# Block moves of a hybrid mixer: issued by ScalarE in its written order, by way of a DRAM scratch of two halves

## The chip, the cores and the metric

The kernel runs on one core of one Trainium2 chip. The metric is the device time of one execution in microseconds; it is given as the median of the runs shown. Times inside a profile are microseconds from the first instruction. TensorE (PE) multiplies matrices, VectorE (DVE), ScalarE (ACT) and GpSimd (POOL) work on elements, SyncE (SP) issues DMAs only.

## The reference

One layer of an encoder block for 256 tokens of width 2048, in float32:

```python
h  = rms_norm(x, pre_mix_g)
P  = h @ w_in                        # u, B, C (1024 each), c_q (768), c_kv (512), k_rope (64)
yA = group_rms_norm(B * conv3_causal(C * u))
q  = rms_norm(c_q) @ w_uq            # 8 heads of 128 + 64
kv = rms_norm(c_kv) @ w_ukv          # 8 heads of 128 + 128
o  = chunk_causal_attention(q_nope, rope(q_rope), k_nope, rope(k_rope), v)
yB = group_rms_norm(o)               # one group for each head
x  = x + rms_norm(concat(yA, yB) @ w_o, post_mix_g)
x  = x + rms_norm(square(relu(rms_norm(x) @ w_up)) @ w_down, post_mlp_g)
```

## The kernel before

**Products.** All weights are streamed once. Each product is made of three matmuls: weights and activations are split into a high part and a rest (`w_hi`, `w_lo`, `xT_hi`, `xT_lo`), and hi*hi, lo*hi and hi*lo are added. The unit is a quad: four chunks of 128 weight rows by 512 columns, 1 MB, loaded by SyncE into one of four `raw` slots (L605). A quad has two halves of two chunks. ScalarE copies a half to `w_hi` (L1005), VectorE subtracts to get `w_lo` (L1305), TensorE does 6 matmuls for each chunk (L725 to L727), 12 for a half. A half is split four halves ahead of its use: the split waits for the end of the half four earlier (`half_used`), and it stands in ScalarE's and VectorE's order at the odd chunk of that earlier half.

**One written order.** `plan()` (L76) writes a single list of steps. Every engine walks the whole list and does its own part of each step, so the list fixes the order on each engine. The first three strips of the input projection make the latents (`lat`), then come 24 quads of u, c and b columns. Before each of their chunks, number `sub`, `between(sub)` (L130) puts the small work of the head pairs and of the convolution. Pair p (0 to 3) begins at step 8 + 16p: kv product, q product (+4), kq turn (+6), `qrT` (+9), `q_order` (+13), scores (+15), probsT (+19), pv (+22), sum of squares and normalisation of o (+24, +25), o turn (+26), `o_split` (+36). So the o turn of pair p stands at step 34 + 16p, and `q_order` and scores of pair p+1 at 37 + 16p and 39 + 16p. Convolution turns stand at 38 and 54.

**Moves of blocks.** Twelve times a 256-token tile has to be transposed without TensorE: 2 latent strips, 4 times k and q, 4 times o, 2 convolution strips. VectorE transposes 32x32 blocks into the one buffer `blk` (`turn_batch`, L1329, `blk_turned`), after the batch before has been stored (`blk_stored`). Then four DMAs store `blk` into `mix_rows` in DRAM (L634), and a fifth reads it back with the blocks in their places (L647, `blk_landed`). SyncE does all this in `move_batch`, called after the load of the fourth quad after the turn. Its waits stand in the same queue as the weight loads. The scratch holds one batch, so the stores wait until the batch before has landed.

**Who waits for a landing.** `lat_split` (L1106) makes cqT from the latents. `q_order` on ScalarE (L1138) waits for the kq batch, copies q into order and raises `qT_ready`; TensorE's score matmuls (L909, L914) wait for it. `o_split` (L1162) and the convolution's steps (L1189) wait for theirs, with many steps in between. In ScalarE's order one split stands between step 35 + 16p and the `q_order` of step 37 + 16p.

Of the kernel before, what the change touches and what calls it, by code (L numbers as in the profile page):

```python
# [27 lines left out]
F32 = mybir.dt.float32  # L28
# [18 lines left out]
BLK = 32  # L47
# [23 lines left out]

S_CONV, S_OUT = 3, 9
CONV_PARTS = "ucb" * 2


def plan():  # L76
# [6 lines left out]
        quads[n] = dict(kind=kind, **kw)  # L83
        return n

    def turn(kind, i):

        batches.append((kind, i, len(quads) + 4))
        steps.append((kind + "_turn", i, len(batches) - 1))

    def products(n, into=steps, then=None):

# [11 lines left out]
    for s in range(3):  # L104
        for q in range(4):
            n = quad("in", strip=s, q=q, nk=4, width=min(W, LAT - s * W), col=LAT0 + s * W,
                     first=q == 0, last=q == 3)
            for k in range(4):
                steps.append(("mm", n, k))
                if s == 0 and q < 2 and k % 2:  # L110
                    c = 8 + 4 * q + 2 * (k // 2)
                    steps += [("xT", c, 0), ("xT", c + 1, 0)]
                if (s, q, k) == (1, 1, 1):
                    steps.append(("x_stats", 0, 0))
                if (s, q, k) == (1, 2, 0):
                    steps.append(("lat_out", 0, lat_ends[0]))
                if (s, q, k) == (1, 2, 1):
                    turn("lat", 0)
                if (s, q, k) == (2, 0, 1):
                    turn("lat", 1)  # L120
                    steps.append(("lat_squares", 0, 0))
                if (s, q, k) == (2, 1, 0):
                    steps.append(("lat_split", 0, 0))
        lat_ends[s] = n
        if s:
            steps.append(("lat_out", s, n))
    steps += [("lat_squares", 1, 0), ("rotatedate", 0, 0)]


    def between(sub):  # L130
        if sub == 2:
            steps.append(("latT", 0, 0))
        if sub == 1:
            steps.append(("lat_split", 1, 0))
        if sub == 6:
            steps.append(("krT", 0, 0))
        if sub in (38, 54):
            turn("conv", sub // 54)
        for p in range(PAIRS):
            at = sub - 8 - 16 * p  # L140
            if at == 0:
                n = quad("kv", p=p, nk=4, width=W)
                products(n)
                steps.append(("kv_out", p, n))
            if at == 4:
                for part in range(2):
                    n = quad("q", p=p, part=part, nk=3, width=QW)
                    products(n)
                steps.append(("q_out", p, n))
            if at == 6:  # L150
                turn("kq", p)
            if at == 26:
                turn("o", p)
            for when, what, h in [(9, "qrT", 0), (13, "q_order", 0), (15, "scores", 0), (15, "scores", 1),
                                  (19, "probsT", 0), (19, "probsT", 1), (22, "pv", 0), (24, "o_squares", 0),
                                  (25, "o_norm", 0), (36, "o_split", 0)]:
                if at == when:
                    steps.append((what, p, h))
        for c in range(4):
            for half, t, norm in [(0, 70 + 6 * c, 8), (1, 98 + 4 * c, 5)]:  # L160
                if sub == t:
                    steps.append(("convT", half, c))
                if sub == t + 2:
                    steps.append(("conv_square", half, c))
                if sub == t + norm:
                    steps.append(("conv_norm", half, c))

    sub = 0
# [73 lines left out]
    n = up(0, 3)  # L242
# [58 lines left out]

def hybrid_block(nc, t, out):
    steps, tail, quads, batches = plan()
    BATCH = {(kind, i): n for n, (kind, i, _) in enumerate(batches)}
    NQ_TAIL = min(n for what, n, _ in tail if what == "mm")
    NQ_ALL = max(quads) + 1
    LOOP = range(2, FF_STRIPS - 2)
# [3 lines left out]
    with ExitStack() as ctx:  # L311
# [197 lines left out]
            k = m - Q_RANK // P  # L509
            return yT_hi[:, KV_AT + k], yT_lo[:, KV_AT + k], G_KV + k  # L510

        mix_rows = nc.dram_tensor("mix_rows", (4, BLK, 4, 8 * BLK), F32, kind="Internal").ap()

        def landed(batch):
            return 16 * (BATCH[batch] + 1)
# [86 lines left out]
        def _(sp):  # L602
# [18 lines left out]
                        sp.dma_start(aT_raw[BLK * q:BLK * (q + 1), g], a_blk[BLK * g:BLK * (g + 1), q]  # L621
                                     ).then_inc(aT_landed, 16)

            def move_batch(m):

                kind, i, _ = batches[m]
                size = 4 * BLK if kind == "o" else 8 * BLK
                sp.wait_ge(blk_turned, m + 1)
                if m:

                    sp.wait_ge(blk_landed, 16 * m)
                for g in range(4):
                    src = blk[BLK * g:BLK * (g + 1)].rearrange("p q b c i -> p q (b c i)")[:, :, 0:size]
                    sp.dma_start(mix_rows[:, :, g, 0:size].rearrange("q r n -> r q n"), src).then_inc(blk_stored, 16)  # L634
                if kind == "kq":
                    sp.wait_ge(latT_lo_ready, 2)
                    if i:
                        sp.wait_ge(scores_done, 2 * i)
                elif kind == "lat" and i:
                    sp.wait_ge(latT_lo_ready, i)  # L640
                elif kind == "o":
                    sp.wait_ge(latT_lo_ready, 3)
                    sp.wait_ge(kr_ready, 4)
                    if i:
                        sp.wait_ge(oT_lo_ready, i)
                sp.wait_ge(blk_stored, 64 * (m + 1))
                sp.dma_start(landing(kind, i), mix_rows[:, :, :, 0:size].rearrange("q r g n -> (q r) g n")  # L647
                             ).then_inc(blk_landed, 16)

            def load_x(tb):  # L650
                sp.dma_start(x_in[:, tb], x_dram[:, tb]).then_inc(x_landed, 16)

# [10 lines left out]
            for n in range(RAW, NQ):  # L663
                z = quads[n]

                sp.wait_ge(lo_ready, 2 * (n - RAW) + 2)
                load_quad(n % RAW, quad_source(n), z["nk"], z["width"])
                if n in (5, 6):
                    load_x(n - 5)
                if n == 7:  # L670
                    sp.dma_start(ident[:], t["ident"]).then_inc(ident_landed, 16)
                    sp.dma_start(cos_t[:], t["cos"]).then_inc(tables_landed, 16)
                    sp.dma_start(sin_t[:], t["sin"]).then_inc(tables_landed, 16)
                for m, (_, _, after) in enumerate(batches):
                    if after == n:
                        move_batch(m)
                if n == RESIDUAL_QUAD:

                    sp.wait_ge(oT_lo_ready, PAIRS)
                    sp.dma_start(g_post_mix[:], t["post_mix_g"].to_broadcast([P, D])).then_inc(g_mix_landed, 16)  # L680
                    sp.dma_start(x_res[:], x_dram).then_inc(x_res_landed, 16)
# [316 lines left out]
        def _(act):  # L998
# [58 lines left out]
            def step(what, a, b):  # L1057
# [64 lines left out]
                elif what == "q_out":  # L1122
# [5 lines left out]
                    for tb in range(TB):  # L1128
                        ins = nc.scalar.activation(q_sb[:, tb], ps[:, 4 + tb, 0:QW], ACT.Copy,  # L1129
                                                   scale=rstd_lat[:, tb:tb + 1])  # L1130
                    ins.then_inc(q_ready, 1)
                elif what == "q_order":
                    act.wait_ge(blk_landed, landed(("kq", a)))
                    if a:
# [697 lines left out]
```

## Time and profile before

| | before |
|---|---|
| median of 3 runs | 1068.28 us (1066.87 to 1068.4) |
| the profiled execution | 1067.39 us |
| its span, first to last instruction | 1065.6 us |
| TensorE busy | 1053.6 us, 99% |
| VectorE busy | 695.2 us, 65% |
| ScalarE busy | 515.9 us, 48% |
| mean granted TensorE clock | 0.997 |

The profile has a page, with busy times and the costliest groups of instructions, and a trace that can be asked for timelines of an engine, for tables of busy time by stretch, and for waits. In a timeline row "x4" means four instructions in a row merged, with their time in common; the brackets give the idle time before and what ended it. "SPq" and "ACTq" are the instructions by which SyncE and ScalarE issue DMAs; their time is that of the issue, not of the transfer, and does not count as busy. Matmuls overlap: their pitch is the distance of their starts. PEclk 1.00 is the full clock of 2.4 GHz.

### The profile page before, as it was taken

The numbers are of one execution on the slowest core, as the hardware profiler recorded it, in microseconds if no ns is written. First come the engines' busy times: TensorE is split into PE (matmuls) and PEld (weight loads), VectorE is DVE, ScalarE is ACT, GpSimd is POOL, SyncE is SP. The second block draws the span as 40 slices with busy tenths as digits, with TensorE's granted clock in tenths as the row PEclk, the third lists the DMA queues.
The fourth block names the chain that finished last, engine by engine and source line by source line (L and its number), as shares of the span: only waits on it lengthen the run. The fifth ranks groups of instructions, "written<-read, shape, count | busy, mean of one in ns | idle before, by whom it ended". The sixth has DMA issues, their size and how long they took to land.

```text
span 1065.6 us, 13494 instructions
## 1 busy us (share of the span) xinstructions
PE 1053.6 (99%) x4794; PEld 877.0 (82%) x4794; DVE 695.2 (65%) x785; ACT 515.9 (48%) x666; POOL 80.7 (8%) x94
## 2 busy tenths in 40 slices
PE   9999999999999999999999999999999999999996
PEld 7898888888888788888888888888888888888885
DVE  6475566679975876575575665756657656565666
ACT  7575545565544664444444444444444444444443
POOL 0011022110000310000000000000000000000003
PEclk9999999999999999999999999999999999999998
DMA  9786667864586465776666756666576665676562
GB/s 345 261 300 218 201 184 272 271 221 151 204 307 198 125 212 157 237 226 197 209 184 212 231 172 232 196 199 212 170 236 216 203 211 159 220 232 190 181 242 79
DMA packets 125619, 225.78 MB, mean 212 GB/s; under 512 B 8464, under 2 KB 30096, under 8 KB 124816
## 3 DMA queue, kind: packets, MB, share of 16 engines
q1 hardware_dynamic: 125152, 224.89, 64.7%
q10 hardware_dynamic: 432, 0.44, 0.1%
q8 instruction: 21, 0.34, 0.1%
q14 instruction: 14, 0.11, 0.0%
HBM read 210.08 MB, written 7.34 MB: 204 GB/s over the span
## 4 chain that ended last, share of the span: by engine, by line
PE 85%; issue 11%; DVE 2%; POOL 1%; DMA 1%; ACT 0%; SPq 0%; DVEq 0%; POOLq 0%; ACTq 0%
PE ps L725 28%; PE ps L727 28%; PE ps L726 28%; DMA raw<-in_w_in 1%; PE ps L748 1%; POOL acc L1666 0%; DVE w_lo L1305 0%; PE ps L909 0%; PE ps L914 0%; POOL x_res L1777 0%; POOL x_res L1751 0%; ACT w_hi L1005 0%; SPq L656 0%; DVE conv_s L1532 0%; DVEq L311 0%
## 5 line engine op out<-in xcount | busy, mean ns | idle before, releaser
L1305 DVE TENSOR_TENSOR w_lo<-raw,w_hi 128x1024 fp32r<-128x1024 f32 (+2 forms) x382 | 465.2, 1226 | 318.9 <-ACT w_hi L1005 316.8
L1005 ACT ACTIVATE w_hi<-raw 128x1024 fp32r<-128x1024 f32 (+2 forms) x382 | 395.8, 1038 | 460.7 <-PE ps L727 456.3
L725 PE MATMUL ps<-w_hi,xT_hi 128*128 128x512 f32 (+1 forms) x792 | 308.5, 390 | 0.6 <-DVE xT_lo L1406 0.5
L727 PE MATMUL ps<-w_lo,xT_hi 128*128 128x512 f32 (+1 forms) x792 | 305.9, 386 | 0.0
L726 PE MATMUL ps<-w_hi,xT_lo 128*128 128x512 f32 (+1 forms) x792 | 305.8, 386 | 0.0
L725 PE MATMUL ps<-w_hi,yT_hi 128*128 128x512 f32 x672 | 263.1, 391 | 0.0
L727 PE MATMUL ps<-w_lo,yT_hi 128*128 128x512 f32 x672 | 261.6, 389 | 0.0
L726 PE MATMUL ps<-w_hi,yT_lo 128*128 128x512 f32 x672 | 261.4, 389 | 0.0
L725 PEld LDWEIGHTS ps<-w_hi,xT_hi 128*128 128x128 f32 x792 | 148.7, 188 | 31.9 <-issue 2.0
L727 PEld LDWEIGHTS ps<-w_lo,xT_hi 128*128 128x128 f32 x792 | 148.6, 188 | 30.0
L726 PEld LDWEIGHTS ps<-w_hi,xT_lo 128*128 128x128 f32 x792 | 148.8, 188 | 28.7
L727 PEld LDWEIGHTS ps<-w_lo,yT_hi 128*128 128x128 f32 x672 | 126.1, 188 | 26.5
L726 PEld LDWEIGHTS ps<-w_hi,yT_lo 128*128 128x128 f32 x672 | 126.2, 188 | 26.1
L725 PEld LDWEIGHTS ps<-w_hi,yT_hi 128*128 128x128 f32 x672 | 126.1, 188 | 25.9
L1379 DVE TENSOR_TENSOR acc<-acc,ps 128x1024 f32<-128x1024 f32 x58 | 70.8, 1220 | 18.4 <-PE ps L727 17.5
L1685 POOL TENSOR_TENSOR a_sb<-a_sb 128x1024 f32<-128x1024 f32 x16 | 30.3, 1895 | 583.0 <-ACT a_sb L1035 583.0
L1035 ACT ACTIVATE a_sb<-ps,rstd_x 128x512 f32<-128x512 f32 x32 | 20.2, 683 | 19.9 <-PE ps L727 19.9
L1325 DVE TENSOR_TENSOR yT_lo<-aT_raw,yT_hi 128x512 fp32r<-128x512 f32 x32 | 20.6, 683 | 0.0
L1350 DVE STREAM_TRANSPOSE a_blk<-a_sb 128x512 f32<-128x512 f32 x30 | 19.5, 687 | 0.0
L1044 ACT ACTIVATE yT_hi<-aT_raw 128x512 fp32r<-128x512 f32 x32 | 18.2, 615 | 1.5 <-DVE aT_raw L1360 1.5
L1672 POOL TENSOR_TENSOR rope_c<-q_sb,cos_t 128x128 f32<-128x128 f32 x8 | 8.6, 1073 | 114.6 <-ACT q_sb L1129 114.3
L727 PE MATMUL ps<-w_lo,cqT_hi 128*128 128x384 f32 x48 | 16.1, 335 | 0.0
(155 smaller groups left out, 425.3 us busy)
## 6 DMA issues: line engine op xcount, KB each, us to landing
raw<-in_w_up SPq DMA_DIRECT2D x64, 1024.0 KB, 5.5
raw<-in_w_down SPq DMA_DIRECT2D x64, 1024.0 KB, 5.3
raw<-in_w_in SPq DMA_DIRECT2D x28, 1024.0 KB, 6.0
raw<-in_w_o SPq DMA_DIRECT2D x16, 1024.0 KB, 5.0
aT_raw<-a_blk SPq DMA_DIRECT2D x240, 32.0 KB, 1.9
raw<-in_w_uq SPq DMA_DIRECT2D x8, 576.0 KB, 4.9
mix_rows<-blk SPq DMA_DIRECT2D x32, 128.0 KB, 2.4
raw<-in_w_ukv SPq DMA_DIRECT2D x4, 1024.0 KB, 5.3
```

The lines of the kernel that those rows point to most:

```text
L725: nc.tensor.matmul(dst, x_hi, hi, start=first, stop=False)
L726: nc.tensor.matmul(dst, x_lo, hi, start=False, stop=False)
L727: mm = nc.tensor.matmul(dst, x_hi, lo, start=False, stop=last)
L748: mm = nc.tensor.transpose(ps[:, bank, i * P:(i + 1) * P], src, ident[:])
L1005: nc.scalar.activation(w_hi[:, slot, 0:size], raw[:, raw_slot, first:first + size], ACT.Copy).then_inc(hi_ready, 1)
L1035: ins = nc.scalar.activation(a_sb[:, tb], ps[:, bank + tb], ACT.Relu, scale=rstd_x2[:, tb:tb + 1])
L1044: ins = nc.scalar.activation(turned(yT_hi, at, tb), blocked(tb), ACT.Copy)
L1305: nc.vector.tensor_tensor(w_lo[:, slot, 0:size], raw[:, raw_slot, first:first + size], f32(w_hi[:, slot, 0:size]), ALU.subtract).then_inc( ...
L1325: ins = nc.vector.tensor_tensor(turned(yT_lo, at, tb), blocked(tb), f32(turned(yT_hi, at, tb)), ALU.subtract)
L1350: ins = nc.vector.transpose(a_blk[:, :, tb].rearrange("p q c i -> p c q i"), a_sb[:, tb].rearrange("p (c q i) -> p c q i", c=4, q=4))
L1379: nc.vector.tensor_tensor(m, m, ps[:, bank:bank + 2], ALU.add).then_inc(acc_added, 1)
L1685: nc.gpsimd.tensor_tensor(a, a, a, ALU.mult).then_inc(a_ready, 1)
```

## The change

SyncE's `move_batch` goes. The list of steps gets two new steps for each batch, `move_store` and `move_read`, and ScalarE carries them out where they stand. For a turn at step `at` the store stands at `at + 1`, the read at `at + 4` (kq), `at + 5` (o) or `at + 6` (conv), each ahead of everything else of that step. For the two latent batches the places are written by hand. The store waits for the turn and issues four DMAs; the read waits as before for the landing place to be free, for the batch before to have landed and for its own stores, and issues one. The scratch `mix_rows` has two halves used in turn, and the wait for the landing of the batch before moves from the store to the read.

```diff
+MOVE = {"kq": 4, "o": 5, "conv": 6}
...
-    def turn(kind, i):
-
-        batches.append((kind, i, len(quads) + 4))
+    moves = {}
+
+    def turn(kind, i, at=None):
+
+        batches.append((kind, i))
         steps.append((kind + "_turn", i, len(batches) - 1))
+        if at is not None:
+            moves.setdefault(at + 1, []).append(("move_store", len(batches) - 1, 0))
+            moves.setdefault(at + MOVE[kind], []).append(("move_read", len(batches) - 1, 0))
...
+                for b, when in enumerate([((1, 2, 3), (1, 3, 3)), ((2, 0, 3), (2, 2, 2))]):
+                    if (s, q, k) in when:
+                        steps.append((("move_store", "move_read")[when.index((s, q, k))], b, 0))
...
     def between(sub):
+        steps.extend(moves.pop(sub, []))
...
-        mix_rows = nc.dram_tensor("mix_rows", (4, BLK, 4, 8 * BLK), F32, kind="Internal").ap()
+        mix_rows = nc.dram_tensor("mix_rows", (2, 4, BLK, 4, 8 * BLK), F32, kind="Internal").ap()
...
-                for m, (_, _, after) in enumerate(batches):
-                    if after == n:
-                        move_batch(m)
...
+                elif what == "move_store":
+                    kind, i = batches[a]
+                    size = 4 * BLK if kind == "o" else 8 * BLK
+                    act.wait_ge(blk_turned, a + 1)
+                    for g in range(4):
+                        src = blk[BLK * g:BLK * (g + 1)].rearrange("p q b c i -> p q (b c i)")[:, :, 0:size]
+                        act.dma_start(mix_rows[a % 2, :, :, g, 0:size].rearrange("q r n -> r q n"), src
+                                      ).then_inc(blk_stored, 16)
+                elif what == "move_read":
...
+                    if kind == "kq":
+                        act.wait_ge(latT_lo_ready, 2)
+                        if i:
+                            act.wait_ge(scores_done, 2 * i)
+                    elif kind == "lat" and i:
+                        act.wait_ge(latT_lo_ready, i)
+                    elif kind == "o":
+                        act.wait_ge(latT_lo_ready, 3)
+                        act.wait_ge(kr_ready, 4)
+                        if i:
+                            act.wait_ge(oT_lo_ready, i)
+                    if a:
+
+                        act.wait_ge(blk_landed, 16 * a)
+                    act.wait_ge(blk_stored, 64 * (a + 1))
+                    act.dma_start(landing(kind, i), mix_rows[a % 2, :, :, :, 0:size].rearrange("q r g n -> (q r) g n")
+                                  ).then_inc(blk_landed, 16)
```

## Rows read from the trace of the kernel before

**Rows 1.** The page's part 1: busy us (share of the span) xinstructions.
```profile
PE 1053.6 (99%) x4794; PEld 877.0 (82%) x4794; DVE 695.2 (65%) x785; ACT 515.9 (48%) x666; POOL 80.7 (8%) x94
```

**Rows 2.** Windows: stretch, its us, busy us of PE, PEld, DVE, ACT, POOL; PEclk, DMA share, GB/s.
```profile
44.00:340.00 296.00, 296.00 (x1445) 251.04 (x1444) 203.82 (x304) 158.27 (x251) 29.24 (x53) 1.00 0.68 228
```

**Rows 3.** Timeline of ScalarE, 0 to 4 us: start, us, engine, line, operation, [idle before].
```profile
1.72 0.39 ACTq L1050 DMA_DIRECT2D xT_raw<-in_xT  x1
...
2.95 0.20 ACT L1055 ACTIVATE rstd_m<-ones 128x2 f32<-128x2 f32 x1
```

**Rows 4.** Timeline of SyncE's queue, pair 1: groups of four stores.
```profile
137.95 1.78 SPq L634 DMA_DIRECT2D mix_rows<-blk  x4
...
146.12 3.37 SPq L634 DMA_DIRECT2D mix_rows<-blk  x4
```

**Rows 5.** Timeline of VectorE, pair 1.
```profile
138.75 1.23 DVE L1305 TENSOR_TENSOR w_lo<-raw,w_hi 128x1024 fp32r<-128x1024 f32 x1 [0.83 <-ACT w_hi L1005]
...
145.38 0.70 DVE L1334 STREAM_TRANSPOSE blk<-o_sb 128x512 f32<-128x512 f32 x1
```

**Rows 6.** Timeline of ScalarE, pair 1: a split, and q_order.
```profile
137.66 1.06 ACT L1005 ACTIVATE w_hi<-raw 128x1024 fp32r<-128x1024 f32 x1 [3.02 <-PE ps L727]
...
145.14 0.72 ACT L1138 ACTIVATE lat<-kqT 128x256 f32<-128x256 f32 x2 [0.72 <-DMA kqT<-mix_rows]
```

**Rows 7.** Timeline of TensorE, pair 1: the first score matmuls.
```profile
147.24 1.47 PE L909 MATMUL ps<-kqT,lat 128*128 128x128 f32 x8
```

**Rows 8.** Timelines of VectorE and TensorE, pairs 2 and 3.
```profile
176.96 1.23 DVE L1305 TENSOR_TENSOR w_lo<-raw,w_hi 128x1024 fp32r<-128x1024 f32 x1 [0.83 <-ACT w_hi L1005]
...
182.28 0.70 DVE L1334 STREAM_TRANSPOSE blk<-o_sb 128x512 f32<-128x512 f32 x1
...
185.44 1.47 PE L909 MATMUL ps<-kqT,lat 128*128 128x128 f32 x8
...
220.48 0.70 DVE L1334 STREAM_TRANSPOSE blk<-o_sb 128x512 f32<-128x512 f32 x1
...
223.65 1.47 PE L909 MATMUL ps<-kqT,lat 128*128 128x128 f32 x8
```

**Rows 9.** Timelines of ScalarE and TensorE, pair 0: q_order and scores.
```profile
107.28 0.73 ACT L1138 ACTIVATE lat<-kqT 128x256 f32<-128x256 f32 x2 [1.06 <-DMA kqT<-mix_rows]
...
109.03 1.47 PE L909 MATMUL ps<-kqT,lat 128*128 128x128 f32 x8
```

**Rows 10.** Timelines of all engines, 51 to 64 us: the latent batches.
```profile
51.79 1.25 ACT L1020 ACTIVATE lat<-ps,rstd_x 128x512 f32<-128x512 f32 x2
...
52.41 0.34 SPq L647 DMA_DIRECT2D kqT<-mix_rows  x1
...
55.77 1.99 SPq L634 DMA_DIRECT2D mix_rows<-blk  x4
...
55.99 1.70 ACT L1106 ACTIVATE cqT_hi<-kqT,gains 128x256 fp32r<-128x256 f32 x4
...
59.83 2.68 DVE L1305 TENSOR_TENSOR w_lo<-raw,w_hi 128x640 fp32r<-128x640 f32 x3
...
61.50 0.31 PE L725 MATMUL ps<-w_hi,xT_hi 128*128 128x320 f32 x1
...
63.38 0.34 SPq L647 DMA_DIRECT2D kqT<-mix_rows  x1
```

**Rows 11.** Timelines of VectorE and TensorE, 249 to 259 us: the last o batch.
```profile
249.59 0.70 DVE L1334 STREAM_TRANSPOSE blk<-o_sb 128x512 f32<-128x512 f32 x1
...
255.66 2.35 DVE L1305 TENSOR_TENSOR w_lo<-raw,w_hi 128x1024 fp32r<-128x1024 f32 x2
...
258.07 0.39 PE L725 MATMUL ps<-w_hi,xT_hi 128*128 128x512 f32 x1
```

**Rows 12.** Windows around TensorE's last matmul, columns as in rows 2.
```profile
1056.00:1060.00 4.00, 0.57 (x3) 0.14 (x1) 3.23 (x6) 1.02 (x3) 3.25 (x3) 1.00 0.66 262
1060.00:1061.00 1.00, 0.00 (x0) 0.00 (x0) 1.00 (x2) 0.00 (x0) 0.00 (x0) 0.54 0.00 0
```

More of the change, by code:

```diff
@@ L137, in between @@
         if sub in (38, 54):
-            turn("conv", sub // 54)
+            turn("conv", sub // 54, sub)
         for p in range(PAIRS):
@@ L150, in between @@
             if at == 6:
-                turn("kq", p)
+                turn("kq", p, sub)
             if at == 26:
-                turn("o", p)
+                turn("o", p, sub)
             for when, what, h in [(9, "qrT", 0), (13, "q_order", 0), (15, "scores", 0), (15, "scores", 1),
@@ L303, in hybrid_block @@
     steps, tail, quads, batches = plan()
-    BATCH = {(kind, i): n for n, (kind, i, _) in enumerate(batches)}
+    BATCH = {(kind, i): n for n, (kind, i) in enumerate(batches)}
     NQ_TAIL = min(n for what, n, _ in tail if what == "mm")
@@ L622, in move_blocks @@
                                      ).then_inc(aT_landed, 16)
[L624 to L648, printed above, removed]
             def load_x(tb):
@@ L1131, in step @@
                     ins.then_inc(q_ready, 1)
+                elif what == "move_store":
[7 more added lines that the diff above has]
+                elif what == "move_read":
+                    kind, i = batches[a]
+                    size = 4 * BLK if kind == "o" else 8 * BLK
+                    if kind == "kq":
[14 more added lines that the diff above has]
+                                  ).then_inc(blk_landed, 16)
                 elif what == "q_order":
```

## The prediction

> **What bounds the kernel now.** I read the page first: TensorE is busy 1053.6 of 1065.6 us, ScalarE 515.9 [rows 1]. Then the table of windows over the stretch in which the twelve batches of blocks are moved: from 44 to 340 us TensorE is busy 296.00 of 296.00 us at full clock, ScalarE 158.27, VectorE 203.82 [rows 2]. So there TensorE alone sets the end, nothing in that stretch can be gained, and every microsecond in which it stands still is a microsecond of the result. Third, the timelines of SyncE, ScalarE, VectorE and TensorE around each batch, to see how much room lies between a thing that TensorE needs and the moment it needs it. Matmuls of 512 columns start 0.227 us apart in TensorE's timeline, so a half quad (two chunks, 12 matmuls) takes 2.72 us. A half is split four halves ahead: ScalarE waits for the end of half H, makes w_hi of H+4, VectorE then w_lo; TensorE asks for it three halves after H.
>
> **What goes from SyncE.** 48 stores and 12 reads leave its queue, and with them its waits for turns and landings. What stands behind them there are weight loads. In the stretch of rows 2 TensorE has no idle time at all, so earlier weights are worth nothing. I cost this at zero; the cover is the four raw slots, and if it were gone weights would only be earlier than now, so no loss either.
>
> **What comes to ScalarE: issue time.** The nearest rows are its own load at the start, 0.39 us, and SyncE's groups of four stores, 1.78 us [rows 3, 4]. So 12 x (4 x 0.44 + 0.4) = about 26 us of ScalarE, spread over some 210 us in which it is about half busy. By total it fits. A load was also issued at 1.72 us while the copy ahead of it in ScalarE's order ran only at 2.95 [rows 3]: an issue need not wait for work queued ahead to finish, only for its semaphores. What counts is therefore the order: a store at one step after the turn waits for VectorE's transposes, and VectorE runs several us behind TensorE. Behind the waiting store stand w_hi splits, and in three of the four head pairs the q_order copy, for which the score matmuls wait.
>
> **Pair 1 worked out.** (a) The kq turn is done when SyncE's stores start, 137.95, and four issues take 1.78 us [rows 4]. ScalarE reaches that step earlier (it is idle 3.02 us before its split at 137.66 [rows 6]), waits, issues until 139.73, and only then makes the split, 2.07 us late. (b) VectorE's w_lo at 138.75 [rows 5] follows that split, so it starts at 139.73 + 1.06 + 0.03 = 140.82, again 2.07 late. Behind it in VectorE's order stand the sum of squares of o, the normalisation (with GpSimd between them) and the o turn, a serial chain: the turn at 145.38 + 0.70 = 146.08 [rows 5] becomes 148.15. (c) The o stores now stand in ScalarE's order ahead of one split and of q_order. ScalarE waits till 148.15, issues 1.77 us (149.96), splits 1.06 (151.02), copies q in 0.73 (151.75) [rows 6]. (d) TensorE began the scores at 147.24 [rows 7], the instant its previous chunk was through; now 151.85. That is a stall of 4.6 us. The kq read is no part of it: its stores have landed when ScalarE comes to it, and its data were there by 145.14 [rows 6]. After the scores ScalarE also waits for the conv turn and issues four stores before it takes the exponentials: by the same steps they end 7.2 us after the scores begin. Weights split before last till three halves and the scores are through (2.4 + 1.36 + 5.44 = 9.2 us), so I put nothing there.
>
> **Pairs 2 and 3.** Same steps; VectorE has no conv product in the chain, so the turn stood earlier against the scores. Pair 2: the w_lo behind the kq turn, 176.96, moves by the same 2.07 to 179.03; the end of the o turn, 182.98, to 185.05; plus 1.77 + 1.06 + 0.73 + 0.05 gives 188.65 against 185.44: 3.2 us. Pair 3: turn end 221.18 + 2.07, plus 3.6, gives 226.85 against 223.65: 3.2 us [rows 8].
>
> **Pair 0** has no o batch ahead of it. The kq stores delay a split and u's copy, the read's stores have landed before, and q_order ran at 107.28 to 108.01 with the scores at 109.03 [rows 9]: 1.0 us of room, against at most 1.3 us of delay if the read had to wait for the splits to finish. I take 0, bound 0.3.
>
> **The two latent batches.** The first batch's read stood at 52.41, and the copy of strip 1 at 51.79 on ScalarE comes behind it now, 1.0 us later; the second turn, which needs that copy, is 1.0 later too (stores from 56.8 where they stood at 55.77). They take 2.0 us, and lat_split, which ran at 55.99, starts at 58.8: 2.8 us later. VectorE's half of it and the first w_lo behind it (59.83 + 0.82 = 60.65) come to 63.5, while TensorE wants that half at 61.50 [rows 10]. Stall 2.0 us. Bounds: 1.0, if the first group of stores lands sooner, so that strip 1's copy is not held up, and 4.0 if both groups go as slowly as the slowest, 3.37 [rows 4].
> On the queues: the stores from 55.77 were followed by their read only 7.6 us later, with a megabyte of weights on the same queue ahead of them [rows 10]. The Trainium skill, "DMA: Bandwidth & Descriptors", Queues, rings and completion order, says that each DMA engine goes round between the queues that have work, a packet at a time; blocks on ScalarE's queue would then not stand behind weights. By that rule the latent stall would be 1.0 and the sum 1 us less; by the row it is 2.0, which I keep.
>
> **The last o batch.** Its turn ends at 250.29. ScalarE issues till 252.1, and its next split is ready at 253.2, where VectorE now has it long before it wants it. In VectorE's order follow that half's w_lo (1.2 us), a convolution's reciprocal and gain (3.0) and the next half's w_lo (1.2), which so ends at 258.6; it started at 255.66 and ended at 256.8. TensorE asks for that half at 258.07 [rows 11]. Stall 0.5, bounds 0 and 1.7, since VectorE is nearly full till 300 us and keeps the lateness. The conv batches' turns are followed by nothing urgent: 0 beside what stands under pair 1.
>
> **Sum.** 2.0 + 0 + 4.6 + 3.2 + 3.2 + 0.5 = 13.5 us. The profiled execution took 1067.39 us (span 1065.6 and 1.8 around it), so 1080.9 by it; it lies 0.9 below the median of the three runs, 1068.28, which gives 1081.8. Nothing is given back later: outside that stretch TensorE's idle time is 12 us in all [rows 1], at the start and the end.
>
> **Rivals.**
> (A) The clock falls in a stall. After the last matmul, at 1056.18, the clock was still 1.00 up to 1060 and 0.54 in the slice from 1060 to 1061 [rows 12]: it drops to its lower level after some 3.5 us of idleness. The stall of pair 1 is longer, the other two about as long. At 1.2 GHz the 0.227 us pitch doubles. No row shows how long it stays low; if as long as it took to fall, each fall costs 1.75 us. One fall: 1083.6; three: 1087. For: 4.6 is above 3.5. Against: 3.2 is below. Chance 0.2.
> The Trainium skill, "TensorE: Matmul & The Clock Gate", Part 1, tells the same: a gate halves the clock once the array has been idle and opens after it has been busy for a while. The rows agree on the fall; the rise is in no row here.
> (B) Issues on ScalarE are slow because SyncE issues weights beside them. The slowest group took 3.37 us [rows 4]; 1.6 more in each of three pairs: 13.5 + 4.8, 1086.6. Chance 0.12.
> (C) VectorE is not shifted by the kq stores (the split gets ahead of them), and only the o stores block: 2.5 + 1.1 + 1.1, and 1 for the latents: 1074. Against it is the written order. Chance 0.12.
> (D) Not slower. The point is the o turn: if it ended 4.6 us earlier against the scores (before 143.6 in pair 1), ScalarE would pass the stores without holding q_order. That could be if the o chain, with SyncE out of the way, ran ahead. Time 1068.3, with no stall left. Against it: the chain is released by ScalarE's splits and by TensorE, and SyncE appears nowhere in it. Chance 0.08.
> Main case: 0.48.
>
> **Numbers.** Forecast 1081.8. The range runs from (C), less 1 us for latents that cost nothing, 1073, to three clock falls or slow issues with a little more in the latent and last batches, 1090; only (D) and a sum of both bad cases is left out. Measurements of this kernel tell 0.2% (2.1 us) from no change. Faster 0.03, same 0.06, slower 0.91.
>
> **What would show it.** TensorE idle just before the score matmuls of line 909 by 4.6, 3.2 and 3.2 us in pairs 1, 2 and 3 and none in pair 0; ScalarE's o stores starting as VectorE's o turn ends, with q_order after them; the w_lo behind each kq turn 2.1 us later against TensorE; an idle time of 2 us in strip 2; the clock below 1.00 in pair 1 for (A). I would be wrong if q_order ran ahead of the o stores, if the stalls were at weights instead of scores, or if TensorE showed none.

## The result, and the profile after

The changed kernel takes 1092.62 us (median of 4 runs, 1091.2 to 1093.26) where the kernel before takes 1067.91 beside it (4 runs): a ratio of 1.023 (95% interval 1.0217 to 1.0243), 24.7 us more. Forecast was 1081.8, with a range to 1090: the direction was right, the size was not, and the time lies outside the range.

| | before | after |
|---|---|---|
| the profiled execution | 1067.39 us | 1091.2 us |
| its span | 1065.6 us | 1089.4 us |
| TensorE busy | 1053.6 us | 1060.2 us |
| TensorE idle in the span | 12.0 us | 29.2 us |
| mean granted clock | 0.997 | 0.993 |

So 23.8 us of span come from two sources: 17.2 us in which TensorE stands still, and 6.6 us by which the same 4794 matmuls are busy longer. The page of the changed kernel: part 1, which answers to [rows 1], and the line of part 3 for ScalarE's queue (packets, MB, share), on which the blocks now travel:

```profile
PE 1060.2 (97%) x4794; PEld 880.3 (81%) x4794; DVE 695.3 (64%) x785; ACT 514.4 (47%) x666; POOL 80.6 (7%) x94
...
q10 hardware_dynamic: 10608, 10.92, 3.5%
```

Two lines of TensorE's waits (us in total, times, longest) hold 16.2 us of the idle time:

```profile
PE ps L890 <- issue: 11.1, 3, 4.6
PE ps L706 <- DVE w_lo L1314: 5.1, 4, 3.4
```

Windows of the changed kernel, columns as in [rows 2], show where it is. Before, TensorE was busy through all of this stretch at full clock [rows 2]:

```profile
44.00:64.00 20.00, 18.75 (x107) 16.86 (x106) 8.40 (x11) 9.68 (x18) 0.58 (x1) 1.00 0.74 213
64.00:92.00 28.00, 24.63 (x116) 21.00 (x115) 18.72 (x33) 16.76 (x28) 3.59 (x9) 0.94 0.65 215
128.00:172.00 44.00, 39.44 (x192) 33.11 (x191) 24.43 (x39) 17.46 (x29) 6.39 (x11) 0.96 0.60 189
172.00:212.00 40.00, 36.76 (x179) 30.70 (x178) 22.82 (x39) 18.19 (x30) 6.39 (x11) 0.96 0.65 214
212.00:264.00 52.00, 48.71 (x248) 41.27 (x247) 33.27 (x57) 27.41 (x47) 7.44 (x12) 1.00 0.69 223
```

The first two are strip 2, where the latent batches are moved: 1.25 + 3.37 = 4.6 us idle. The other three hold the score matmuls of pairs 1, 2 and 3: 4.56, 3.24 and 3.29. The clock column is below 1.00 in three of the five. TensorE's timeline has the same stalls one by one (start, us, operation, idle before and what ended it); the last two rows are those behind the last o batch:

```profile
59.87 0.42 PE L706 MATMUL ps<-w_hi,xT_hi 128*128 128x320 f32 x1 [0.85 <-DVE w_lo L1314]
62.29 0.41 PE L706 MATMUL ps<-w_hi,xT_hi 128*128 128x320 f32 x1 [0.40 <-DVE w_lo L1314]
67.69 0.64 PE L706 MATMUL ps<-w_hi,xT_hi 128*128 128x320 f32 x1 [3.37 <-DVE w_lo L1314]
159.59 2.90 PE L890 MATMUL ps<-kqT,lat 128*128 128x128 f32 x8 [4.56 <-issue]
202.76 2.00 PE L890 MATMUL ps<-kqT,lat 128*128 128x128 f32 x8 [3.24 <-issue]
246.04 1.55 PE L890 MATMUL ps<-kqT,lat 128*128 128x128 f32 x8 [3.29 <-issue]
281.16 0.50 PE L706 MATMUL ps<-w_hi,xT_hi 128*128 128x512 f32 x1 [0.49 <-DVE w_lo L1314]
298.24 0.67 PE L938 MATMUL ps<-conv_s,ones 128*128 128x256 f32 x2 [0.40 <-ACT conv_s L1204]
```

Eight score matmuls took 1.47 us before [rows 7]; behind the stall of pair 1 they take 2.90. Slices of 2 us around it, same columns, show why: the clock falls near the end of the stall and comes back some 3.4 us later (a slice at c spends 2(1-c)/0.5 us low: 0.64 + 2.00 + 0.76).

```profile
156.00:158.00 2.00, 0.00 (x0) 0.00 (x0) 0.00 (x0) 0.18 (x1) 0.00 (x0) 1.00 0.42 90
158.00:160.00 2.00, 0.41 (x2) 0.44 (x3) 1.09 (x1) 2.00 (x4) 0.00 (x0) 0.84 0.20 42
160.00:162.00 2.00, 2.00 (x8) 1.59 (x7) 1.67 (x3) 0.44 (x1) 0.00 (x0) 0.50 0.57 161
162.00:164.00 2.00, 2.00 (x13) 1.17 (x12) 1.30 (x6) 0.00 (x0) 0.00 (x0) 0.81 0.99 346
```

ScalarE's timeline in pair 1 tells why `q_order` comes late. The o turn (VectorE's, 155.20 + 0.70) ends at 155.90; only then are the four stores issued, then the split, then q:

```profile
145.59 1.78 ACTq L1119 DMA_DIRECT2D mix_rows<-blk  x4
...
155.93 1.79 ACTq L1119 DMA_DIRECT2D mix_rows<-blk  x4
157.82 1.06 ACT L986 ACTIVATE w_hi<-raw 128x1024 fp32r<-128x1024 f32 x1 [8.34 <-DMA mix_rows<-blk]
158.78 0.71 ACT L1147 ACTIVATE lat<-kqT 128x256 f32<-128x256 f32 x2
```

TensorE was through with its weights at 155.03. What stands in the way is thus the order on ScalarE, as forecast. The latent batches are another matter. ScalarE's timeline of the first of them:

```profile
48.66 3.12 ACTq L1119 DMA_DIRECT2D mix_rows<-blk  x4
56.62 0.34 ACTq L1139 DMA_DIRECT2D kqT<-mix_rows  x1
57.07 1.27 ACT L1001 ACTIVATE lat<-ps,rstd_x 128x512 f32<-128x512 f32 x2 [3.81 <-DMA mix_rows<-blk]
```

SyncE's timeline beside it, three loads of weights from 45.65 to 54.61; they start at 45.65, 49.37 and 54.25, so the last two go out between the first store and the read:

```profile
45.65 8.96 SPq L615 DMA_DIRECT2D raw<-in_w_in  x3
```

The read in the table of DMAs from 45 to 62 us (KB, us from issue to landing):

```profile
kqT<-mix_rows ACTq DMA_DIRECT2D x1, 512.0 KB, 6.3
```

From the first store to the read 8.0 us pass, and the read lands 6.3 us later. In the kernel before, SyncE's timeline has the stores here:

```profile
47.80 2.77 SPq L634 DMA_DIRECT2D mix_rows<-blk  x4
```

and the same table of DMAs has the read:

```profile
kqT<-mix_rows SPq DMA_DIRECT2D x1, 512.0 KB, 3.3
```

Its read followed at 52.41 [rows 10], 4.6 us after the first store, and SyncE issued no weights in between. In the changed kernel they go out beside the stores, ahead of the read. Loads behind a read do no such harm: the second latent read of the changed kernel, at 68.05, had none issued in the 5.8 us ahead of it and one 0.34 us behind it, and landed in 3.5 us; the read of before at 52.41 had loads 0.39 and 0.87 us behind it.

### The profile page after: what moved, and what is told of

Same layout as the page of the kernel before. It is cut to its first block, busy times and chain, and to the rows that moved or that the text cites. A ratio compares the mean times of both kernels' runs of the same rounds, so it can differ in the third digit from the quotient of the medians.

```text
span 1089.4 us, 13489 instructions
## 1 busy us (share of the span) xinstructions
PE 1060.2 (97%) x4794; PEld 880.3 (81%) x4794; DVE 695.3 (64%) x785; ACT 514.4 (47%) x666; POOL 80.6 (7%) x94
## 4 chain that ended last, share of the span: by engine, by line
PE 81%; issue 12%; DVE 2%; ACT 1%; DMA 1%; POOL 1%; ACTq 0%; SPq 0%; DVEq 0%; POOLq 0%
PE ps L706 26%; PE ps L708 26%; PE ps L707 26%; PE ps L890 1%; DMA raw<-in_w_in 1%; DVE w_lo L1314 1%; PE ps L729 1%; DMA mix_rows<-blk 1%; POOL acc L1675 0%; ACT w_hi L986 0%; PE ps L895 0%; ACTq L1119 0%; POOL x_res L1786 0%; POOL x_res L1760 0%; DVE cqT_lo L1348 0%
## 5 line engine op out<-in xcount | busy, mean ns | idle before, releaser
L890 PE MATMUL ps<-kqT,lat 128*128 128x128 f32 (+1 forms) x32 | 7.9, 402 | 11.1 <-issue 11.1
```

What stands on the lines that cost most here:

```text
L890: nc.tensor.matmul(ps[:, (6, 7)[h], cols], qT[:, tb, h], kT, start=tb == 0, stop=False, skip_group_check=True)
```

## The experiments

Theory at the start: (T1) the order on ScalarE makes the stalls, by the o stores ahead of `q_order` and by the kq stores that make the o turn late; (T2) SyncE's waits had held weight loads back, and freed loads run against the blocks; (T3) the clock falls in the stalls. The rival to T1 is the time of issuing on ScalarE as such, that to T2 the order of the latent steps, that to T3 that the slow matmuls have another cause. The kernels `only_o`, `only_kq` and `lat_sync` keep SyncE's old `move_batch` for the kinds named in `BY_SYNC`; all of them keep the scratch of two halves.

**only_o: the four o batches by ScalarE, all others by SyncE.**

```diff
+BY_SYNC = ('lat', 'kq', 'conv')
...
-        if at is not None:
+        if at is not None and kind not in BY_SYNC:
...
+                for m, (kind, _, after) in enumerate(batches):
+                    if after == n and kind in BY_SYNC:
+                        move_batch(m)
```

> Only the four o batches are issued by ScalarE, at the changed kernel's places; latent, kq and conv batches stay with SyncE. Theory (order: the o stores stand ahead of q_order and hold it until VectorE's o turn): the chain without the kq shift of 2.07 us gives idle times of TensorE ahead of the scores of 2.5, 1.1 and 1.1 us in pairs 1 to 3, no fall of the clock, and 0.5 us at the last batch: 5 us above before, 1073. Rival 1 (time of issue: each batch costs in proportion): 4 of 12 batches cost a third of 24.7, 8 us, 1076, with no idle time tied to scores. Rival 2 (the kq stores alone do it): 1068.

Measured 1075.85 us, ratio 1.007 (1.0053 to 1.0087). Windows of pairs 1 and 2:

```profile
128.00:172.00 44.00, 41.58 (x203) 35.21 (x202) 27.18 (x44) 19.95 (x33) 6.40 (x11) 0.96 0.67 218
172.00:212.00 40.00, 38.89 (x196) 32.97 (x196) 25.18 (x43) 19.52 (x33) 6.40 (x11) 1.00 0.72 231
```

TensorE's timeline in pairs 2 and 3:

```profile
191.61 1.55 PE L920 MATMUL ps<-kqT,lat 128*128 128x128 f32 x8 [1.11 <-issue]
231.44 1.55 PE L920 MATMUL ps<-kqT,lat 128*128 128x128 f32 x8 [1.39 <-issue]
```

The stalls are 2.42, 1.11 and 1.39 (4.9 in all), against 2.5, 1.1 and 1.1 by the prediction's steps without the shift by the kq stores. Above the forecast lies first the clock: 0.96 in pair 1, after a stall of only 2.42 us. Not all of the 3.6 us by which TensorE is busy longer is the clock's, though. From the scores of pair 2 to those of pair 3, with no fall, 39.83 us pass, 1.39 of them the stall; that leaves 38.44, where it was 38.21 before [rows 8]. So a stall costs some 0.2 us beside its own length.

**only_kq: the kq batches by ScalarE, all others by SyncE** (the edit above with `BY_SYNC = ('lat', 'o', 'conv')`).

> Only the four kq batches are issued by ScalarE, at the changed kernel's places; the rest stays with SyncE. Theory: VectorE's o turns come 2.07 us later, as in the changed kernel, but nobody on TensorE's side waits for them, so no idle time ahead of the scores: within 1 us of before, 1068. Rival 1 (time of issue): a third of 24.7, 1076. Rival 2 (the kq stores hold q_order by themselves): idle times ahead of the scores in pair 0 too, 3 us or more in all, 1071 and up.

Measured 1068.09 us over 10 runs, ratio 1.0003 (0.9993 to 1.0012). The window of pair 1 has no idle time:

```profile
128.00:172.00 44.00, 44.00 (x222) 37.62 (x221) 30.45 (x47) 22.29 (x36) 6.88 (x12) 1.00 0.69 230
```

although in VectorE's timeline the o turn came at 147.79, where it stood at 145.38 [rows 5]:

```profile
147.79 0.70 DVE L1373 STREAM_TRANSPOSE blk<-o_sb 128x512 f32<-128x512 f32 x1
```

The issue time of 20 DMAs on ScalarE costs nothing by itself: that rival falls. The kq stores do harm only where the o stores wait for the turn that they make late: 0 and 4.9 us of stall alone, 11.1 together.

**o_late: the o store three steps later, its read two.**

```diff
-MOVE = {"kq": 4, "o": 5, "conv": 6}
+MOVE = {"kq": 4, "o": 7, "conv": 6}
+STORE = {"kq": 1, "o": 4, "conv": 1}
...
-            moves.setdefault(at + 1, []).append(("move_store", len(batches) - 1, 0))
+            moves.setdefault(at + STORE[kind], []).append(("move_store", len(batches) - 1, 0))
```

> The changed kernel with the o stores three steps later, at +4 after the turn and so behind the next pair's q_order, and the o reads at +7. Theory: the three idle times ahead of the scores (4.56, 3.24, 3.29 us, together 11.1) go, and with them two falls of the clock, 1.7 us each. In their place VectorE's conv turn waits for the o stores and the conv stores come later, ahead of the exponentials: some 1.5 us of waits at weights in pair 1. 1092.6 - 11.1 - 3.4 + 1.5 = 1079.6. Rival (the time of issue or the number of waits on ScalarE counts, not the place): no change, 1092.

Measured 1085.74 us, ratio 1.0167 (1.015 to 1.0184). No stall is left at the scores, but others came. VectorE's timeline in pair 1, and TensorE's:

```profile
163.59 1.31 DVE L1344 STREAM_TRANSPOSE blk<-u_sb 128x512 f32<-128x512 f32 x2 [5.70 <-DMA mix_rows<-blk]
```

```profile
170.78 0.80 PE L707 MATMUL ps<-w_hi,xT_hi 128*128 128x512 f32 x1 [4.06 <-DVE w_lo L1315]
```

The conv turn stands behind the o turn and needs `blk` empty. It now waited 5.70 us for the o stores; the softmax behind it on VectorE, and the splits behind that, came late. So a store can stand too late as well as too early, since there is one `blk`. The expectation had this wait, but at some 1.5 us of stalls in pair 1, and no fall of the clock; it was 4.06 us with a fall behind it, and further stalls of 1.48 and 1.53 us stand at 213.59 and 284.76.

**kq_late: the kq store one step later**, behind the split (`STORE = {"kq": 2, "o": 1, "conv": 1}`).

> The changed kernel with the kq stores one step later, at +2 after the turn, behind the split that they stood ahead of. Theory: that split is no longer late, VectorE's o turn comes 2.07 us earlier against TensorE, and the idle times ahead of the scores become 2.5, 1.1 and 1.1 us; two falls of the clock go too: 1092.6 - 6.4 - 3.4 = 1082.8. Rival (the o turn is late for another cause, such as DMAs beside it): idle times as in the changed kernel, 1092.

Measured 1083.05 us, ratio 1.0139 (1.0122 to 1.0156). TensorE's waits, and its timeline in pair 1:

```profile
PE ps L891 <- issue: 4.8, 4, 2.4
```

```profile
158.00 1.61 PE L891 MATMUL ps<-kqT,lat 128*128 128x128 f32 x8 [2.39 <-issue]
```

The stalls at the scores go from 11.1 to 4.8 us (0.32 in pair 0, then 2.39, 1.05, 1.06), those of `only_o`. The 2 us by which the kq stores delay a split, and with it the o turn, are thereby shown in each pair. That the time meets the 1082.8 expected is in part luck: of the two falls of the clock that were to go, the one in pair 1 stayed (0.96 from 128 to 172, behind 2.39 us), and the profiled execution is only 7.5 us below that of the changed kernel, where 9.8 were expected.

**lat_sync: only the two latent batches back to SyncE** (`BY_SYNC = ('lat',)`).

> The changed kernel with the two latent batches back at SyncE; kq, o and conv batches stay with ScalarE. Theory (parts add up): the idle times of TensorE in strip 2, 0.85 + 0.40 + 3.37 us, go, and the fall of the clock there, 1.7 us by the other falls; the score idle times stay: 1092.6 - 4.6 - 1.7 = 1086.3. Rival (the latent batches only shift work that is late anyway): under 2 us of gain, 1091.

Measured 1086.43 us, ratio 1.0169 (1.0146 to 1.0192). Windows, columns as in [rows 2]:

```profile
44.00:92.00 48.00, 48.00 (x256) 42.84 (x255) 29.33 (x47) 29.43 (x48) 3.59 (x9) 1.00 0.76 246
128.00:172.00 44.00, 39.44 (x185) 32.63 (x184) 25.13 (x40) 17.26 (x30) 6.39 (x11) 0.92 0.62 194
172.00:212.00 40.00, 36.75 (x169) 30.34 (x168) 22.65 (x38) 17.46 (x29) 6.39 (x11) 0.91 0.63 202
212.00:264.00 52.00, 48.73 (x237) 40.82 (x236) 33.26 (x56) 26.43 (x45) 7.43 (x12) 0.93 0.61 200
```

The 4.6 us in strip 2 are gone, the idle times of the pairs are within 0.02 us those of the changed kernel, and the clock fell in all three of them, for about 7 us each time (44 x 0.08/0.5, 40 x 0.09/0.5, 52 x 0.07/0.5). The median says less than it seems: two of the four runs took 1084 us and two, the profiled one among them, 1088.8, at granted clocks of 0.993 to 0.995 and of 0.989.

**gate: the changed kernel, but SyncE waits for the latent landings** after its 12th and 14th load, so that no more weights are under way beside them. This tells T2 from the order of the steps, which it leaves alone.

```diff
+LAT_LOADS = (11, 13)
...
+                for m, when in enumerate(LAT_LOADS):
+                    if n == when:
+                        sp.wait_ge(blk_landed, 16 * (m + 1))
```

> The changed kernel with one wait added on SyncE: after its 12th and 14th quad load it waits for the first and second latent batch to have landed, as it did by its own moves before. ScalarE still issues all moves. Theory (weights that SyncE no longer holds back run beside the first batch's stores and make them land 8 us after their issue instead of 4.6): the read goes out some 3 us earlier, the idle time in strip 2 is the 2.0 us of the prediction, the fall of the clock there goes: 1092.6 - 2.6 - 1.7 = 1088.3. Rival (ScalarE's own queue is slower by itself): idle time 4.6 as before, 1092.

Measured 1087.53 us, ratio 1.0196 (1.0179 to 1.0213). ScalarE's timeline, the table of DMAs from 45 to 62 us, and TensorE's timeline in strip 2:

```profile
48.27 2.76 ACTq L1123 DMA_DIRECT2D mix_rows<-blk  x4
52.87 0.34 ACTq L1143 DMA_DIRECT2D kqT<-mix_rows  x1
```

```profile
kqT<-mix_rows ACTq DMA_DIRECT2D x1, 512.0 KB, 3.1
```

```profile
64.11 0.41 PE L710 MATMUL ps<-w_hi,xT_hi 128*128 128x320 f32 x1 [2.12 <-DVE w_lo L1318]
```

From store to read 4.6 us again, as before the change, and the read lands in 3.1. The stall is 2.12, the 2.0 of the prediction. Of the 4.6 us in strip 2 the order thus makes 2.1, the weights beside the blocks 2.5. The clock stays at 1.00 in strip 2. Elsewhere it did not repeat the changed kernel: it fell in pair 1 for about 7 us (0.92 from 128 to 172), not in pair 2 behind a stall of 3.24 us, and in pair 3 behind one of 3.27.

**busy: 8, 6 and 6 dummy matmuls, whose product nothing uses, ahead of the scores of pairs 1 to 3**, while TensorE waits. It should keep the clock up.

The other waits of the scores move ahead of them (left out here).

```diff
+                    for _ in range((0, 8, 6, 6)[p]):
+                        nc.tensor.matmul(ps[:, 6, 3 * P:4 * P], ones[:], ones[:], start=True, stop=True)
                     pe.wait_ge(blk_landed, landed(("kq", p)))
                     pe.wait_ge(qT_ready, p + 1)
```

> The changed kernel with 8, 6 and 6 extra 128x128 matmuls of the ones tile on TensorE ahead of the scores of pairs 1, 2 and 3, in an unused part of the bank; they run while TensorE would stand idle, so the wait itself stays. Theory (the clock falls because TensorE is idle, and the low stretch after it costs some 1.7 us each in pairs 1 and 2): scores start at the same distance, clock 1.00 there, 1092.6 - 3.4 = 1089.2. Rival (the low clock costs nothing, its matmuls would wait anyway): 1092.6.

Measured 1093.29 us, ratio 1.0241 (1.0224 to 1.0258). It tells nothing of T3: the eight took 1.95 us in all, 2.82 of the wait stayed idle, and the clock fell all the same (0.50 in the slice from 160 to 162). I had sized them too small.

**busy2: the same with 18, 13 and 13.**

> As the kernel with 8, 6 and 6 extra matmuls, but with 18, 13 and 13. Eight of them took only 1.95 us there, 0.24 us each, and left TensorE idle for 2.8 us, and the clock fell all the same. Now 4.4, 3.2 and 3.2 us are filled, so almost nothing of the idle time stays. Theory (idleness makes the clock fall and the low stretch costs time): clock 1.00 in pairs 1 to 3, scores at the same distance, some 4 us less than the changed kernel, 1089. Rival (the low clock costs nothing): 1092.6.

Measured 1089.08 us, ratio 1.0199 (1.0181 to 1.0217). The window of pair 1, and TensorE's timeline in it (each dummy is two instructions):

```profile
128.00:172.00 44.00, 43.25 (x233) 37.35 (x232) 25.50 (x42) 17.62 (x30) 6.40 (x11) 1.00 0.61 188
```

```profile
155.82 4.18 PE L885 MATMUL ps<-ones 128*128 128x128 f32 x36
160.75 1.00 PE L892 MATMUL ps<-kqT,lat 128*128 128x128 f32 x5 [0.75 <-ACT lat L1149]
```

The clock is 1.00 in all three pairs, and the median is 3.5 us below that of the changed kernel. What a fall is worth is better read inside the profiles, since the runs of one kernel differ in their falls. The scores of pairs 1, 2 and 3 start at 160.75, 202.46 and 244.26 here, 41.71 and 41.80 us apart, where the changed kernel, with a fall behind each, has 43.17 and 43.28: 1.5 us for each fall. (The profiled executions are only 1.8 us apart, because strip 2 of this one has 1.1 us more of idle time.)

**halves: the kernel before with the scratch of two halves and the wait for the batch before moved to the read**, all by SyncE.

```diff
-                if m:
-                    sp.wait_ge(blk_landed, 16 * m)
...
-                    sp.dma_start(mix_rows[:, :, g, 0:size].rearrange("q r n -> r q n"), src).then_inc(blk_stored, 16)
+                    sp.dma_start(mix_rows[m % 2, :, :, g, 0:size].rearrange("q r n -> r q n"), src).then_inc(blk_stored, 16)
...
+                if m:
+                    sp.wait_ge(blk_landed, 16 * m)
```

> The kernel before, SyncE issuing everything, with the scratch of two halves alone and the wait for the landing of the batch before moved from store to read. Theory: batches rarely follow each other closely and TensorE has no idle time there: within 1 us of before, 1068. Rival (the second half or the moved wait costs, by slower landings): over 1070.

Measured 1067.66 us over 10 runs, ratio 1.0001 (0.9992 to 1.0011). This part of the change costs and gives nothing.

**placed: ten batches on ScalarE, at other places; the latents by SyncE.** The kq store stands behind the split (but in pair 0), the o store behind `q_order`, and the conv turns four steps later, so that they don't wait for `blk`.

```diff
-MOVE = {"kq": 4, "o": 5, "conv": 6}
+STORE = {"kq": 2, "o": 4, "conv": 1}
+MOVE = {"kq": 4, "o": 7, "conv": 5}
...
-        if sub in (38, 54):
-            turn("conv", sub // 54, sub)
+        if sub in (42, 58):
+            turn("conv", sub // 58, sub)
```

> Ten of twelve batches issued by ScalarE, in other places: kq stores at +2 after the turn (pair 0 at +1), o stores at +4 and their reads at +7, the conv turns at steps 42 and 58, behind the scores, with the store at +1 and the read at +5; the latent batches with SyncE. Theory (the place in ScalarE's order costs the time, not the issue): no idle time ahead of scores or weights, 1068 to 1069. Rival (some 22 us of issue time on ScalarE and the waits cost by themselves): above 1072.

Measured 1074.27 us, ratio 1.0062 (1.0044 to 1.008), not the 1068 to 1069 expected. Pairs 0 to 2 have at most 0.15 us of stall at the scores, so the time is not what the rival says, that of the issues by themselves. Pair 3 has a stall of another kind, and 1.3 us more stand at 273.10, ahead of transposes of the convolution. TensorE's timeline, and the table of DMAs from 204 to 228 us, in which its read is about as slow as that of the latents was:

```profile
226.95 1.38 PE L921 MATMUL ps<-kqT,lat 128*128 128x128 f32 x6 [2.51 <-DMA kqT<-mix_rows]
```

```profile
kqT<-mix_rows ACTq DMA_DIRECT2D x1, 512.0 KB, 5.7
```

Here again a load of weights had gone out ahead of the read, 3.25 us before it. The same holds in pairs 1 and 2, with loads 2.15 and 2.37 us ahead and landings of 3.9 and 4.3 us.

**placed_all: the same with the latents on ScalarE too**, the first read, the second store and its read placed later, and the waits of `gate` on SyncE.

```diff
-                for b, when in enumerate([((1, 2, 3), (1, 3, 3)), ((2, 0, 3), (2, 2, 2))]):
+                for b, when in enumerate([((1, 2, 3), (2, 0, 1)), ((2, 1, 3), (2, 3, 1))]):
```

> As the kernel with ten batches placed anew, and the two latent batches with ScalarE too: the first read at the second chunk of strip 2, the second store behind lat_split and its read at chunk (2, 3, 1), and SyncE waiting for their landings after its 12th and 14th quad load. Theory: lat_split has only the first read ahead of it and stays where it was, 1068 to 1070. Rival (ScalarE cannot hold a batch in that stretch, where it has backlog from the squares): 2 us or more of idle time in strip 2, 1071 and up.

Measured 1074.83 us, ratio 1.0076 (1.0057 to 1.0094), above the 1070 expected. Strip 2 has 0.41 us of idle time (47.59 of 48.00 busy), so places can be found for the latents as well; pair 3 waits 1.4 us for its read, and the conv transposes 1.2.

**placed_gate: placed, with SyncE waiting for each kq landing.**

```diff
+                    elif after == n and kind == "kq":
+                        sp.wait_ge(blk_landed, 16 * (m + 1))
```

> As the kernel with ten batches placed anew (latents with SyncE), and SyncE waits, after the quad load after which it moved the kq batch before, until ScalarE's kq batch has landed. In the kernel without that wait TensorE stood idle 2.51 us ahead of the scores of pair 3, whose read took 5.7 us to land beside weight loads (3.3 in the kernel before), and the clock fell once. Theory (weights that SyncE no longer holds back slow the moves): the read lands in 3.3 us, that idle time and the fall go, 1.3 us before a transpose of the convolution stay: 1074.3 - 2.5 - 1.7 = 1070. Rival (ScalarE's queue is slower by itself, or q_order is late for another cause): 1074.

Measured 1071.28 us, ratio 1.0039 (1.0024 to 1.0055). The table of DMAs from 204 to 228 us, and TensorE's timeline:

```profile
kqT<-mix_rows ACTq DMA_DIRECT2D x1, 512.0 KB, 3.3
```

```profile
270.90 0.30 PE L762 MATMUL ps<-ident,u_sb 128*128 128x128 f32 x1 [2.19 <-issue]
```

The read of pair 3 lands in 3.3 us again, and its stall is gone: T2 a second time, in another place. A stall of 2.19 us at the conv product's transposes, with the clock at 0.97 from 264 to 320, remains, where 1.3 us were expected. VectorE is busy 47.5 of these 56 us; that it is late there, and by which of the moved steps, was not shown. No kernel of this study is below the one before, nor was one to be expected: in that stretch TensorE had nothing to give [rows 2].

## Why the prediction came out as it did

**The order in the pairs: right, step by step.** Idle before the scores 4.56, 3.24, 3.29 us against 4.6, 3.2, 3.2; none in pair 0. The steps inside hold too: the w_lo behind the kq turn starts 2.98 us after the kq stores (148.57 and 145.59), where it started 0.80 after them [rows 4, 5], so it is 2.2 late against 2.07 forecast; the o turn ends 0.87 after TensorE is ready for the scores, where it ended 1.16 before [rows 5, 7], so it moves by 2.03. (In the prediction's pair 1, 148.15 + 1.77 is 149.92 and not 149.96; it changes nothing.) Nothing was lost behind the scores either: the four waits for w_lo, 5.1 us in all, are the three in strip 2 and the one at 281 us. `only_o`, `only_kq` and `kq_late` show that both halves of this are needed.

**The last o batch: right in size.** 0.49 + 0.40 us against 0.5, within 0 to 1.7.

**The latents: 4.6 us against 2.0, and above the bound of 4.0.** The step that failed is the first one, "What goes from SyncE". It asked whether earlier weights help TensorE and whether they could be late, and answered no to both, rightly. It did not ask what else earlier weights do. SyncE's waits for turns and landings had kept weight loads back from a batch's first store until its read was issued. Without these waits the loads go out beside the blocks, and the blocks, which someone waits for, take longer: 8.0 us from store to read in place of 4.6, 6.3 to land in place of 3.3. `gate` puts the wait back and finds the 2.1 us of the order alone: lat_split, forecast at 58.8, starts at 59.38 there and at 62.97 in the changed kernel. The price was 2.5 us of stall. In the pairs it was nothing: there the last load lay 7.6 us or more ahead of each kq read, and the reads landed in 3.2 to 3.4 us.
The prediction had named a rule by which the latents would cost 1.0 us, and kept to the row. The Trainium skill, "DMA: Bandwidth & Descriptors", Queues, rings and completion order, says that engines go round between queues; that a block on its own queue is then sooner through, was my inference from it. The first batch, on which the stall hung, went the other way, 8.0 us against 4.6, since the row of before had no new weights between store and read. The second, from which the rule was argued, gained little: 7.0 us from store to read (61.06 to 68.05) against 7.6. The same page, under "Issuing engines are not separate DMA queues", says that DMAs of all issuing engines share the same 16 DMA engines and interleave, and that a second issuing engine saves little but issue time. The trace agrees: 6.3 us against 3.3 for the same 512 KB.

**The clock: rival A, which was given 0.2, came true.** This is the second step that failed, and the larger term: the main sum puts the clock at nothing. It was argued away by a single row, the fall after the last matmul [rows 12], read as a length of idleness that a stall must pass. The runs don't bear such a reading: in `only_o` the clock fell with a stall of 2.42 us, in `kq_late` with 2.39, in `placed` with 2.51; in the changed kernel it fell with 4.56 and 3.24 but not with 3.29, in `gate` with 3.27 but not with 3.24. With stalls of 3 to 5 us in three pairs, at least one fall belonged in the main case. From the scores of pair 1 to those of pair 2 the changed kernel takes 43.17 us, 3.24 of them the stall; that leaves 39.93 against 38.20 before [rows 7, 8], 1.73 more, and from pair 2 to 3 it is 1.78 more in the same way. Some 0.2 of each comes with any stall (`only_o`), so a fall costs 1.5 us, as by `busy2`; rival A had 1.75. In `lat_sync`, with 7 us at the low clock, the same distances are 2.9 us longer, so 2.7 for each fall. The price was nearly right, the chance was not. Of the 6.6 us of longer busy time the three falls thus make some 4.6 (an estimate, with the fall in strip 2 priced as the other two); the other 2.0 come with the eight stalls of the table and the start, and the prediction has no term for them. Rival A's last branch, three falls and the stalls of the main case, gave 1087, and with the latents as measured it would have been 1090.
The Trainium skill, "TensorE: Matmul & The Clock Gate", Part 1, says that the gate opens again after the array has been busy; the rise, which no row of before showed, is in the slices of the changed kernel: 0.50, 0.81, and 1.00 from 164 us.

**What is left.** The sum now reads 13.5 + 2.6 (latents) + 0.4 (last batch) + 6.6 (TensorE busy longer, mostly by the clock) = 23.1 of 23.8. The rest, 0.65, lies ahead of 44 us, where TensorE was busy 40.97 us in place of 41.63; kernels of this study that are alike there have 41.05 to 42.05 (`placed_gate`, `placed`), so I give it no cause. The median lies 1.4 above the profiled execution: the other three runs of the changed kernel have spans of 1090.5 to 1091.5 at granted clocks of 0.990 to 0.992, where the profiled one has 0.993.

**The other rivals.** (B), slow issues, fell: a group of four o stores took 1.79 us, not 3.37 (only the first latent group was slow, 3.12). (C) fell: the shift by the kq stores is there. (D), not slower, fell: VectorE's o chain did not run ahead, as SyncE appears nowhere in it.

## What to carry to other kernels

When an engine that also computes is to issue DMAs, compare for each issue the time at which its semaphore rises with the time at which the next thing behind it is needed; here a turn that ended 0.87 us too late, and stores ahead of one copy, made stalls of 3 to 5 us, while twenty issues with nothing urgent behind them cost nothing. A wait in a queue of DMAs may be doing useful work by holding other transfers back: before it goes, ask what will now be under way when the transfer that someone waits for is issued. And a stall of TensorE such as these, of 2 to 5 us, may cost 1.5 to 2.7 us more by its clock, and from one run of a kernel to the next it may or may not.

## What the runs showed of the hardware

- The 512 KB reads of latents and of k and q landed in 3.1 to 3.9 us in all kernels of this study where the last load of weights ahead of them had been issued 5.5 us earlier or more, even with the next one issued less than 0.9 us behind them. With a load issued 2.1 to 4.1 us ahead they took 3.2 to 6.5 us, though they stood on another queue (changed kernel 6.3; `kq_late` 6.5, 3.2, 3.7, 4.1, 4.9; `placed` 3.9, 4.3, 5.7).
- The granted clock fell with stalls of TensorE of 2.19 to 4.56 us, and did not with others of 2.12 and 3.24 (`gate`) and 3.29 us (changed kernel): between these lengths the stall alone does not tell. It stayed low some 3.4 us in the changed kernel, and about 7 us each time in `lat_sync`, with the same stalls; the cost was 1.5 and 2.7 us.
- Matmuls of 128 columns, run while it waits, kept the clock at 1.00 when they left at most 0.75 us of the wait idle, and did not when they left 2.82 (`busy2`, `busy`).
